# Two layers of three-way attention and a recurrent block on one core: the drains of queries, keys and gates are split in two

## The chip, the cores and the metric

The kernel runs on one core of one Trainium2 chip. The metric is the device time of one execution in microseconds. Engines are named by what they do: TensorE (PE in the rows; its weight loads are PEld), VectorE (DVE), ScalarE (ACT), GpSimd (POOL) and SyncE (SP). TensorE writes into PSUM, which this kernel uses as eight banks of 128 x 512 f32.

## The reference, cut to what matters

x is 512 tokens by 1024. Two layers run a projection into queries, keys, values and gates for three kinds of attention, each gated by silu, and a projection back; then a second block with a linear recurrence, dilated attention and a feed-forward part follows, which the change doesn't touch.

```python
def hybrid_layer(x, w_in, f_bias, lam_vec, subln, w_out, g_pre, g_post, layer_idx, cos, sin):
    h = rms_norm(x, g_pre)
    p = h @ w_in
    qa, ka, va, ga, qs, ks, vs, gs, qf, kf, vf, gf, ff = jnp.split(p, split_at, axis=-1)
    ...
    ya = merge(diff_attention(qa, ka, heads(va, ...), lam, lambda_init, subln))
    ya = ya * jax.nn.silu(ga)
    yb = merge(stick_breaking_attention(heads(qs, ...), heads(ks, ...), heads(vs, ...)))
    yb = yb * jax.nn.silu(gs)
    ...
    yc = merge(forgetting_attention(heads(qf, ...), heads(kf, ...), heads(vf, ...), cum_log_f))
    yc = yc * jax.nn.silu(gf)
    y = jnp.concatenate([ya, yb, yc], axis=-1) @ w_out
    return x + rms_norm(y, g_post)
```

## The kernel before

All heavy products are "dense groups". A group multiplies 512 tokens by a weight panel into four tiles of 128 x 512, one in each of the banks 0 to 3. It consists of blocks of 256 rows of the weights; every f32 operand is held as a high and a low part, so a block takes three products for each of its two row chunks and each tile, 24 in all (L644 to L646 with the tokens, L647 to L649 with the weights held in the array). A block's weights come by DMA on SyncE's queue, ScalarE makes the high part (L899) and GpSimd the low part (L627), two blocks ahead.

When the last block of a group is done the group is *drained*: ScalarE and, for some groups, VectorE read the four banks. For queries and keys of the kinds sb and fox (tag `qk`, two groups of four tiles a kind: query pair, key pair, query pair, key pair) ScalarE copies the high part (`qk_high`, L1013 and L1016) and VectorE then subtracts it to get the low part (`qk_low`, L1368 and L1372) and frees the bank. For gates (tag `g`) ScalarE alone applies silu (L980); that needs another activation table than the attention around it, so a table load stands before the first gate, and L1003 loads the attention's table back behind the last. The next group's first product into a bank waits until that bank is free.

The order of the work on every engine comes from one list of steps, `STEPS`, written by `plan()`; each engine walks the list and issues its part of each step, in order. `weave` mixes the blocks of the dense groups, cut into halves of two tiles (tiles 0 and 1, tiles 2 and 3), with the half-steps of an attention. Attention step n has part 0 (scores of unit n into banks 4 and 5, softmax or sticks, turning of unit n - 1, map 0) and part 1 (turning of unit n - 1, map 1, and at some steps the heads). Turned probabilities all pass one bank, 6 (`BT`): TensorE turns into it (L771), ScalarE copies the high part (L1069), VectorE subtracts the low part (L1463) and frees it, and only then TensorE may turn the next. In the kind diff ScalarE copies alone (L1075), exponentials are L1051, the combination L1452. Outputs pass one bank as well, 7 (`BO`): products with the values (L788), the turning of the heads (L823), and VectorE's `y_tmp` (L1532), which frees it for the next. L813 are row factors of fox, and need bank 7 too.

The fourteen groups that the change concerns are, in each of the two layers, `g` of the kinds diff, sb and fox, and `qk` m=0 and m=1 of sb and fox. The time in the trace of layer 0 is given beside them: g diff 118 us, qk sb m=0 198, qk sb m=1 257, g sb 290, qk fox m=0 320, qk fox m=1 390, g fox 433. Layer 1 follows 502 us later.

Of the kernel before, what the change touches and what calls it, by code (L numbers as in the profile page):

```python
# [40 lines left out]

HEADS_AT = {"diff": (10, 13, 16, 18), "sb": (11, 12, 14, 17), "fox": (13, 14, 15, 17), "dil": (8, 13, 17, 18)}
ATT_STEPS = {"diff": 19, "sb": 18, "fox": 18, "dil": 19}
NORM_CHUNKS = (range(DC // 2), range(DC // 2, DC))
S0, S1, BT, BO = 4, 5, 6, 7
MASKS = ("causal", "strict", "chunk", "prev", "mod4d", "mod4", "mod16d", "mod16")
# [2 lines left out]
def plan():  # L49

    groups, steps, blocks = [], [], []

    def dense(tag, rows, orient, **more):

        g = dict(tag=tag, n=rows // BC, orient=orient, index=len(groups), first=len(blocks), **more)
        groups.append(g)
        out = []
        for k in range(g["n"]):
            out.append(("block", len(blocks), len(groups) - 1, k, (0, 1, 2, 3)))
            blocks.append((len(groups) - 1, k))  # L60
        out.append(("drain", len(groups) - 1))
        return out

    def weave(segments, others):

        out, at = [], 0
        for dense_steps, upto in segments:
            rest = [half for st in dense_steps
                    for half in ([st[:4] + ((0, 1),), st[:4] + ((2, 3),)] if st[0] == "block" else [st])]
            n, seen = sum(st[0] == "block" for st in rest), 0  # L70
            for i, other in enumerate(others[at:upto]):
                while rest and (seen < math.ceil(n * (i + 1) / (upto - at)) or rest[0][0] != "block"):
                    seen += rest[0][0] == "block"
                    out.append(rest.pop(0))
                out.append(other)
            out += rest
            at = upto
        return out
# [106 lines left out]
    for st in steps:  # L185
        if st[0] == "drain":
            g = groups[st[1]]
            for j in range(4):
                take(("dense", st[1], j), j, signal=j < 3)
                if g["tag"] == "qk" and g["orient"] == "feat":  # L190
                    mark("qk_high", (st[1], j))
                if g["tag"] == "v" and g["kind"] != "diff":
                    mark("v_high", (st[1], j))
        elif st[0] == "normturn":
            for c in NORM_CHUNKS[st[2]]:
                take(("norm", st[1], c), 4 + c % 4)
        elif st[0] == "forget":
            take(("ff", st[1]), S0)
        elif st[0] == "ropeturn":
            for j in range(4):  # L200
                take(("rope", st[1], j), 4 + j)
                if groups[st[1]]["tag"] == "qk":
                    mark("qk_high", (st[1], j))
        elif st[:2] == ("lru", "decide"):
            take(("r", st[2]), 4 + 2 * (st[2] % 2))
            take(("i", st[2]), 5 + 2 * (st[2] % 2))
        elif st[0] == "att":
            _, l, kind, n, part = st
            turn, value = n - 1, n - 2
            if 0 <= turn < 16:  # L210
                for a in value_maps(kind):
                    if (a > 0) == part:
                        take(("T", l, kind, turn, a), (BT, 0, 1)[a] if kind == "dil" else BT)
                        if kind in ("sb", "fox"):
                            mark("p_high", (l, kind, turn, a))
            if n < 16 and part == 0:
                for a in unit_maps(kind):
                    take(("S", l, kind, n, a), (S0, S1, 3)[a])
                if kind in ("diff", "fox"):
                    for a in range(2):  # L220
                        mark("rows_max", (l, kind, n, a))
                if kind == "dil":
                    mark("rows_max", (l, kind, n, 0))
                if kind == "sb":
                    for a in range(2):
                        mark("sticks", (l, kind, n, a))
                if kind == "diff":
                    mark("soft", (l, kind, n, 1))
            if kind in ("sb", "fox"):
                for p, a in pair_at(n, part):  # L230
                    use[("map", l, kind, p, a)] = maps
                    maps += 1
                    take(("O", l, kind, p, a), BO, signal=False)
                    mark("y_half", (l, kind, p, a))
            elif 0 <= value < 16 and part == 0:
                for a in value_maps(kind):
                    use[("map", l, kind, value, a)] = maps
                    maps += 1
                take(("O", l, kind, value), BO, signal=False)
                if kind == "diff":  # L240
                    mark("rms", (l, kind, value))
            if kind == "fox" and factors_at(n, part) is not None:
                take(("R", l, kind, factors_at(n, part)), BO)
            if n in HEADS_AT[kind] and part == 1:
                p = HEADS_AT[kind].index(n)
                if kind in ("sb", "fox"):
                    mark("gated", (l, kind, p))
                else:
                    take(("Y", l, kind, p), BT if kind == "dil" else BO)
                mark("y_high", (l, kind, p))  # L250
                mark("y_low", (l, kind, p))
# [28 lines left out]
def build(nc, x, wstream, w_ff, f_bias, lam_vec, subln, gains, post_gains, masks, ident_in, sel_in, rope1, positions,  # L280
# [255 lines left out]
    def values_before(gi):  # L536

        n = 0
        for st in STEPS:
            if st == ("drain", gi):  # L540
                return n
            if st[0] == "att" and st[2] in ("sb", "fox"):
                n += len(pair_at(*st[3:]))
            elif st[0] == "att" and 0 <= st[3] - 2 < 16 and st[4] == 0:
                n += len(value_maps(st[2]))
# [48 lines left out]
    with nc.Block() as block:  # L594
# [290 lines left out]
        def _(act):  # L885
# [60 lines left out]
                act.wait_ge(s_lam_dots, l + 1)  # L946
                nc.scalar.activation(lam[:, 2:4], lam[:, 0:2], ACT.Exp).then_inc(s_lam_exp, 1)

            def drain(gi):
                g = GROUPS[gi]  # L950
                tag = g["tag"]
                if tag in ("o", "mix", "o2", "down"):
# [8 lines left out]
                        act.wait_ge(*full(("rope", before[-1], 3)))  # L961
                if tag == "g" and (g["l"], g["ki"]) != (0, 0):
                    act.wait_ge(s_y_low, MARKS["y_low", prev_kind(g["l"], g["kind"]) + (3,)])
                for j in range(4):
                    act.wait_ge(*tile_full(gi, j))
                    ps = bank[j]
                    done = freed(("dense", gi, j))
# [195 lines left out]
            for st in STEPS:  # L1163
# [1 line left out]
                    if st[4][0] == 0:  # L1165
                        high(st[1] + 2)
                elif st[0] == "drain":
                    drain(st[1])
                    if st[1] + 1 in LAST:
                        first_half(LAST.index(st[1] + 1))  # L1170
                elif st[0] == "norm":
# [58 lines left out]
        def _(dve):  # L1230
# [72 lines left out]
                    .then_inc(s_ck_ready, 1)  # L1303
                dve.wait_ge(s_ck_ready, l + 1)

            def drain(gi, tiles=range(4)):
                g = GROUPS[gi]
                tag = g["tag"]
                if tag == "qk" and g["orient"] == "feat":
                    for j in range(4):  # L1310
                        qk_low(g, j, ("dense", gi, j))
                    return
                if tag == "v" and g["kind"] != "diff":
# [327 lines left out]
            for st in STEPS:  # L1641
                if st[0] == "drain":
                    if st[1] not in LAST:
                        drain(st[1])
                elif st[0] == "norm":
                    norm(st[1])
                elif st[0] == "normturn":
# [160 lines left out]
```

## Time and profile before

| what | value |
|---|---|
| median of 3 runs | 1998.19 us (1995.54 to 2000.15) |
| the profiled execution | 1998.55 us, its span 1996.7 us |
| TensorE, busy | 1897.4 us, 95% of the span |
| ScalarE, busy | 906.2 us, 45% |
| VectorE, busy | 778.3 us, 39% |
| GpSimd, busy | 661.8 us, 33% |
| mean granted clock of TensorE | 0.988 |

The busy time of TensorE counts pipelined products whose ends are modelled, so 95% is not 95% of its peak. A row's idle time is the time in which the engine stood still just before, and behind the arrow stands what it was waiting for. Two products that follow each other without a wait start 0.23 us apart at 512 columns and full clock.

### The profile page before, as it was taken

The numbers are of one execution on the slowest core, as the hardware profiler recorded it, in microseconds if no ns is written. First come the engines' busy times: TensorE is split into PE (matmuls) and PEld (weight loads), VectorE is DVE, ScalarE is ACT, GpSimd is POOL, SyncE is SP. The second block draws the span as 40 slices with busy tenths as digits, with TensorE's granted clock in tenths as the row PEclk, the third lists the DMA queues.
The fourth block names the chain that finished last, engine by engine and source line by source line (L and its number), as shares of the span: only waits on it lengthen the run. The fifth ranks groups of instructions, "written<-read, shape, count | busy, mean of one in ns | idle before, by whom it ended". The sixth has DMA issues, their size and how long they took to land.

```text
span 1996.7 us, 24926 instructions
## 1 busy us (share of the span) xinstructions
PE 1897.4 (95%) x9233; PEld 1546.8 (77%) x9239; DVE 778.3 (39%) x1346; ACT 906.2 (45%) x1775; POOL 661.8 (33%) x278
## 2 busy tenths in 40 slices
PE   8998999898999899989899999999999999999998
PEld 6887777676788777777676888888788878888886
DVE  3434655534543565544447672010350431111002
ACT  4555565543465556554353833233453353323222
POOL 2422333122242222322233444434103423444442
PEclk9998999999999899999999999999999999999999
DMA  4221212112322121211231222222102422222322
GB/s 153 85 74 43 74 65 74 53 43 106 116 85 66 51 72 66 74 53 43 104 138 65 95 95 95 86 94 89 60 1 75 142 78 97 95 95 95 99 101 85
DMA packets 44568, 163.74 MB, mean 82 GB/s; under 512 B 6192, under 2 KB 6448, under 8 KB 43824
## 3 DMA queue, kind: packets, MB, share of 16 engines
q1 hardware_dynamic: 42640, 148.65, 22.3%
q10 hardware_dynamic: 1824, 13.63, 1.8%
q8 instruction: 74, 1.21, 0.2%
q14 instruction: 30, 0.25, 0.0%
HBM read 155.97 MB, written 6.29 MB: 81 GB/s over the span
## 4 chain that ended last, share of the span: by engine, by line
PE 82%; DVE 9%; ACT 6%; issue 3%; DMA 0%; POOL 0%; DVEq 0%; ACTq 0%; POOLq 0%; SPq 0%
PE bank L644 12%; PE bank L646 12%; PE bank L645 12%; PE bank L647 10%; PE bank L649 10%; PE bank L648 10%; PE bank L771 2%; PE bank L788 2%; ACT q_dup L1013 2%; PE bank L749 1%; PE bank L747 1%; PE bank L750 1%; DVE y_tok L1398 1%; PE bank L735 1%; PE bank L708 1%
## 5 line engine op out<-in xcount | busy, mean ns | idle before, releaser
L627 POOL TENSOR_TENSOR w_hl<-w_raw,w_hl 128x1024 fp32r<-128x1024 f32 x274 | 661.6, 2419 | 1310.6 <-ACT w_hl L899 1310.0
L899 ACT ACTIVATE w_hl<-w_raw 128x1024 fp32r<-128x1024 f32 x274 | 287.6, 1058 | 343.7 <-DMA w_raw<-wstream 343.2
L644 PE MATMUL bank<-act_hl,w_hl 128*128 128x512 f32 x1056 | 428.4, 406 | 5.7 <-DVE q_low L1368 2.8
L646 PE MATMUL bank<-act_hl,w_hl 128*128 128x512 f32 x1056 | 415.4, 393 | 0.0
L645 PE MATMUL bank<-act_hl,w_hl 128*128 128x512 f32 x1056 | 415.1, 393 | 0.0
L647 PE MATMUL bank<-w_hl,act_hl 128*128 128x512 f32 x672 | 265.6, 395 | 6.1 <-DVE q_low L1368 4.0
L649 PE MATMUL bank<-w_hl,act_hl 128*128 128x512 f32 x672 | 262.3, 390 | 0.0
L648 PE MATMUL bank<-w_hl,act_hl 128*128 128x512 f32 x672 | 262.0, 390 | 0.0
L644 PEld LDWEIGHTS bank<-act_hl,w_hl 128*128 128x128 f32 x1056 | 201.1, 190 | 48.9 <-issue 5.7
L646 PEld LDWEIGHTS bank<-act_hl,w_hl 128*128 128x128 f32 x1056 | 200.2, 190 | 43.5
L645 PEld LDWEIGHTS bank<-act_hl,w_hl 128*128 128x128 f32 x1056 | 201.1, 190 | 40.3 <-issue 1.9
L647 PEld LDWEIGHTS bank<-w_hl,act_hl 128*128 128x128 f32 x672 | 126.3, 188 | 33.9 <-issue 4.9
L649 PEld LDWEIGHTS bank<-w_hl,act_hl 128*128 128x128 f32 x672 | 126.2, 188 | 26.7
L648 PEld LDWEIGHTS bank<-w_hl,act_hl 128*128 128x128 f32 x672 | 126.4, 188 | 24.9
L1069 ACT ACTIVATE pt_hl<-bank 128x512 fp32r<-128x512 f32 (+3 forms) x128 | 55.9, 437 | 177.8 <-PE bank L771 177.5
L1463 DVE TENSOR_TENSOR pt_hl<-bank,pt_hl 128x512 fp32r<-128x512 f32 (+3 forms) x128 | 62.6, 489 | 162.7 <-ACT pt_hl L1069 162.6
L771 PE MATMUL bank<-ident,probs 128*128 128x128 f32 x508 | 89.6, 279 | 29.7 <-DVE pt_hl L1463 29.7
L1424 DVE TENSOR_REDUCE nmax<-bank 128x1 f32<-128x512 f32 (+3 forms) x128 | 59.3, 488 | 89.9 <-PE bank L758 86.8
L771 PEld LDWEIGHTS bank<-ident,probs 128*128 128x128 f32 x508 | 59.3, 142 | 40.7 <-DVE pt_hl L1463 34.2
L1354 DVE TENSOR_TENSOR probs<-bank,probs 128x512 f32<-128x512 f32 x22 | 15.1, 688 | 186.7 <-PE bank L646 186.7
L1396 DVE TENSOR_TENSOR y_tok<-probs,rope 128x256 f32<-128x256 f32 x10 | 4.3, 426 | 196.0 <-ACT probs L969 196.0
L1051 ACT ACTIVATE probs<-bank,nmax 128x256 f32<-128x256 f32 (+3 forms) x144 | 73.2, 515 | 14.8 <-DVE nmax L1424 14.0
(232 smaller groups left out, 2839.7 us busy)
## 6 DMA issues: line engine op xcount, KB each, us to landing
w_raw<-wstream SPq DMA_DIRECT2D x274, 512.0 KB, 3.5
x_spill<-x_res ACTq DMA_DIRECT2D x2, 2048.0 KB, 7.0
x_res<-x_spill ACTq DMA_DIRECT2D x2, 2048.0 KB, 7.9
x_res<-x SPq DMA_DIRECT2D x4, 512.0 KB, 5.7
g_post<-post_gains ACTq DMA_DIRECT2D x4, 512.0 KB, 3.6
x_res<-x ACTq DMA_DIRECT2D x1, 2048.0 KB, 8.4
out<-x_res SPq DMA_DIRECT2D x4, 512.0 KB, 2.6
probs<-w_gates ACTq DMA_DIRECT2D x1, 1024.0 KB, 10.7
```

Of the source, the lines that this page charges most:

```text
L627: nc.gpsimd.tensor_tensor(w_hl[:, slot, 1].rearrange("p c n -> p (c n)"), w_raw[:, slot, :], w_hl[:, slot, 0].rearrange("p c n -> p (c n)" ...
L644: pe.matmul(out_ap, wh, ah, start=start, stop=False)
L645: pe.matmul(out_ap, wh, al, start=False, stop=False)
L646: return pe.matmul(out_ap, wl, ah, start=False, stop=stop)
L647: pe.matmul(out_ap, ah, wh, start=start, stop=False)
L648: pe.matmul(out_ap, ah, wl, start=False, stop=False)
L649: return pe.matmul(out_ap, al, wh, start=False, stop=stop)
L771: tr = pe.transpose(to[:, kb * P:(kb + 1) * P], probs[:, p_slot(kind, n, a), kb * P:(kb + 1) * P], ident[:, :])
L899: nc.scalar.activation(w_hl[:, b % RING, 0].rearrange("p c n -> p (c n)"), w_raw[:, b % RING, :], ACT.Copy).then_inc(s_high_done, 1)
L1051: nc.scalar.activation(ps if in_bank else row, ps, ACT.Exp, bias=nmax[:, par, b:b + 1], accum_out=sums[:, par, a:a + 1])\
L1424: nc.vector.tensor_reduce(nmax[:, par, a:a + 1], ps[:, 0:nb * P], AX.X, ALU.max, negate=True)\
L1463: nc.vector.tensor_tensor(turned_part(1, a, i), ps.rearrange("p (k q) -> p k q", q=P), turned_part(0, a, i).bitcast(f32), ALU.subtract).th ...
```

## The change

The drain of a `qk` or `g` group inside a woven stretch is one step before. It becomes two: tiles 0 and 1 are drained right behind the half of the last block that fills them, before the attention half-step that stands between the block's halves; tiles 2 and 3 are drained behind the second half, where all four were drained before. Drains of other groups and outside `weave` stay whole.

```diff
+SPLIT_DRAINS = ("qk", "g")
...
-        out.append(("drain", len(groups) - 1))
+        out.append(("drain", len(groups) - 1, (0, 1, 2, 3)))
+        return out
+
+    def halves(st):
+
+        return [st[:-1] + ((0, 1),), st[:-1] + ((2, 3),)] if st[0] in ("block", "drain") else [st]
+
+    def halved(dense_steps):
+
+        out = []
+        for st in dense_steps:
+            if st[0] == "drain" and groups[st[1]]["tag"] in SPLIT_DRAINS:
+                first, second = halves(st)
+                out[-1:] = [first, out[-1], second]
+            else:
+                out += halves(st) if st[0] == "block" else [st]
         return out
...
-            rest = [half for st in dense_steps
-                    for half in ([st[:4] + ((0, 1),), st[:4] + ((2, 3),)] if st[0] == "block" else [st])]
+            rest = halved(dense_steps)
...
-            for j in range(4):
+            for j in st[2]:
                 take(("dense", st[1], j), j, signal=j < 3)
...
-            if st == ("drain", gi):
+            if st[:2] == ("drain", gi):
...
-            def drain(gi):
+            def drain(gi, tiles):
...
-                for j in range(4):
+                for j in tiles:
                     act.wait_ge(*tile_full(gi, j))
...
-                    drain(st[1])
+                    drain(st[1], st[2])
...
-            def drain(gi, tiles=range(4)):
+            def drain(gi, tiles):
...
-                    for j in range(4):
+                    for j in tiles:
                         qk_low(g, j, ("dense", gi, j))
```

The last lines of ScalarE's `drain`, which load the attention's table back behind the gates of a drain step, are not changed, so they run once for each of the two steps. TensorE's own order of instructions is the same before and after.

ScalarE at the gates of the kind diff in layer 0, before. L899 is the high part of a weight block, `gate` the gates from banks 0 to 3, L1075 the copy of turned probabilities in the attention step behind:

```order
L899 ACTIVATE w_hl_53<-w_raw_54 128x1024
L980 ACT_TABLE_LOAD
L980 ACTIVATE gate_63<-bank0 128x512
L980 ACTIVATE gate_63<-bank1 128x512
L980 ACTIVATE gate_63<-bank2 128x512
L980 ACTIVATE gate_63<-bank3 128x512
L1003 ACT_TABLE_LOAD
L1075 ACTIVATE probs_55<-bank6 128x128
```

The same place in the changed kernel, where the lines of the kernel have moved down by 15:

```order
L914 ACTIVATE w_hl_53<-w_raw_54 128x1024
L995 ACT_TABLE_LOAD
L995 ACTIVATE gate_63<-bank0 128x512
L995 ACTIVATE gate_63<-bank1 128x512
L1018 ACT_TABLE_LOAD
L995 ACT_TABLE_LOAD
L995 ACTIVATE gate_63<-bank2 128x512
L995 ACTIVATE gate_63<-bank3 128x512
L1018 ACT_TABLE_LOAD
L1090 ACTIVATE probs_55<-bank6 128x128
```

Nothing of the attention has moved between the halves here; a load back and a load forth stand between them.

VectorE at the queries and keys of sb, m=0, in layer 0 (the end of the diff attention), before. `y_tmp` is taken out of bank 7 for head 2 and, at the end, head 3:

```order
L1532 SCALAR_TENSOR_TENSOR y_tmp_58<-bank7,sub_g_94,gate_63 128x512
L1536 TENSOR_TENSOR y_hl_59<-y_tmp_58,y_hl_59 128x512
L1481 TENSOR_SCALAR y_tok_57<-bank7,stat_107 128x128
L1368 SCALAR_TENSOR_TENSOR q_low_67<-bank0,q_dup_64 64x512 x2
L1372 TENSOR_TENSOR k_hl_68<-bank1,k_hl_68 64x512 x2
L1368 SCALAR_TENSOR_TENSOR q_low_67<-bank2,q_dup_64 64x512 x2
L1372 TENSOR_TENSOR k_hl_68<-bank3,k_hl_68 64x512 x2
L1532 SCALAR_TENSOR_TENSOR y_tmp_58<-bank7,sub_g_94,gate_63 128x512
```

And in the changed kernel:

```order
L1383 SCALAR_TENSOR_TENSOR q_low_67<-bank0,q_dup_64 64x512 x2
L1387 TENSOR_TENSOR k_hl_68<-bank1,k_hl_68 64x512 x2
L1547 SCALAR_TENSOR_TENSOR y_tmp_58<-bank7,sub_g_94,gate_63 128x512
L1551 TENSOR_TENSOR y_hl_59<-y_tmp_58,y_hl_59 128x512
L1496 TENSOR_SCALAR y_tok_57<-bank7,stat_107 128x128
L1383 SCALAR_TENSOR_TENSOR q_low_67<-bank2,q_dup_64 64x512 x2
L1387 TENSOR_TENSOR k_hl_68<-bank3,k_hl_68 64x512 x2
L1547 SCALAR_TENSOR_TENSOR y_tmp_58<-bank7,sub_g_94,gate_63 128x512
```

The low parts of tiles 0 and 1 have moved ahead of head 2's `y_tmp`.

ScalarE at the queries and keys of fox, m=1, in layer 0, before. `pt_hl` are copies of turned probabilities out of bank 6, `raw_fox` half of an output out of bank 7, `probs` exponentials:

```order
L899 ACTIVATE w_hl_53<-w_raw_54 128x1024
L1069 ACTIVATE pt_hl_56<-bank6 128x512
L1091 ACTIVATE raw_fox_66<-bank7 64x512
L1069 ACTIVATE pt_hl_56<-bank6 128x3x128
L1051 ACTIVATE probs_55,sums_108<-bank4,nmax_109 128x256
L1051 ACTIVATE probs_55,sums_108<-bank5,nmax_109 128x256
L1013 ACTIVATE q_dup_64<-bank0 64x512 x4
L1016 ACTIVATE k_hl_68<-bank1 64x512 x2
L1013 ACTIVATE q_dup_64<-bank2 64x512 x4
L1016 ACTIVATE k_hl_68<-bank3 64x512 x2
L1069 ACTIVATE pt_hl_56<-bank6 128x384
```

And in the changed kernel:

```order
L914 ACTIVATE w_hl_53<-w_raw_54 128x1024
L1028 ACTIVATE q_dup_64<-bank0 64x512 x4
L1031 ACTIVATE k_hl_68<-bank1 64x512 x2
L1084 ACTIVATE pt_hl_56<-bank6 128x512
L1106 ACTIVATE raw_fox_66<-bank7 64x512
L1084 ACTIVATE pt_hl_56<-bank6 128x3x128
L1066 ACTIVATE probs_55,sums_108<-bank4,nmax_109 128x256
L1066 ACTIVATE probs_55,sums_108<-bank5,nmax_109 128x256
L1028 ACTIVATE q_dup_64<-bank2 64x512 x4
L1031 ACTIVATE k_hl_68<-bank3 64x512 x2
L1084 ACTIVATE pt_hl_56<-bank6 128x384
```

Six activations have moved ahead of two copies of turned probabilities, a half output and the exponentials; six stay ahead of the third copy.

## Rows read from the trace of the kernel before

**Rows 1.** The page, part 4: the chain that ended last, by engine.
```profile
PE 82%; DVE 9%; ACT 6%; issue 3%; DMA 0%; POOL 0%; DVEq 0%; ACTq 0%; POOLq 0%; SPq 0%
```

**Rows 2.** TensorE's waits over the span: us in total, times, longest.
```profile
PE bank L647 <- DVE q_low L1368: 8.4, 8, 1.6
```

**Rows 3.** Groups by line and shape: xcount, busy us, mean ns, idle before.
```profile
L1013 ACT ACTIVATE q_dup<-bank 64x512 fp32r<-64x512 f32 x96 | 56.8, 592 | 13.7 <-PE bank L735 12.5
...
L1372 DVE TENSOR_TENSOR k_hl<-bank,k_hl 64x512 fp32r<-64x512 f32 x48 | 33.0, 688 | 1.1
```

**Rows 4.** Timeline at the diff gates: start us, us, engine, line, idle before.
```profile
121.70 0.60 ACT L980 ACTIVATE gate<-bank 128x512 f32<-128x512 f32 x1 [0.40 <-PE bank L646]
122.31 1.28 ACT L1003 ACT_TABLE_LOAD   x1
123.61 0.28 ACT L1075 ACTIVATE probs<-bank 128x128 f32<-128x128 f32 x1
...
127.05 0.44 PE L749 MATMUL bank<-k_hl,q_dup 128*128 128x384 f32 x1 [0.54 <-DVE probs L1452]
```

**Rows 5.** Timeline at the queries and keys of sb, m=0.
```profile
193.71 1.05 ACT L899 ACTIVATE w_hl<-w_raw 128x1024 fp32r<-128x1024 f32 x1
...
196.08 0.75 DVE L1532 SCALAR_TENSOR_TENSOR y_tmp<-bank,sub_g,gate 128x512 f32<-128x512 f32 x1 [1.82 <-PE bank L823]
...
196.88 0.49 PE L788 MATMUL bank<-vv,probs 128*128 128x128 f32 x2 [0.84 <-DVE y_tmp L1532]
...
202.20 0.47 PE L647 MATMUL bank<-w_hl,y_hl 128*128 128x512 f32 x1 [1.64 <-DVE q_low L1368]
```

**Rows 6.** Timeline at the queries and keys of sb, m=1.
```profile
257.14 0.49 ACT L1069 ACTIVATE pt_hl<-bank 128x384 fp32r<-128x384 f32 x1 [0.50 <-PE bank L771]
...
260.24 0.39 PE L771 MATMUL bank<-ident,probs 128*128 128x128 f32 x2
261.50 0.47 PE L644 MATMUL bank<-act_hl,w_hl 128*128 128x512 f32 x1 [0.87 <-DVE q_low L1368]
...
265.06 0.50 PE L644 MATMUL bank<-act_hl,w_hl 128*128 128x512 f32 x1 [0.54 <-DVE q_low L1368]
```

**Rows 7.** Timeline at the queries and keys of fox, m=0.
```profile
319.32 0.60 ACT L1069 ACTIVATE pt_hl<-bank 128x512 fp32r<-128x512 f32 x1 [1.97 <-PE bank L771]
...
322.55 0.50 PE L771 MATMUL bank<-ident,probs 128*128 128x128 f32 x3
...
324.52 0.47 PE L647 MATMUL bank<-w_hl,act_hl 128*128 128x512 f32 x1 [1.48 <-DVE q_low L1368]
```

**Rows 8.** Timeline at the queries and keys of fox, m=1.
```profile
385.42 0.60 ACT L1069 ACTIVATE pt_hl<-bank 128x512 fp32r<-128x512 f32 x1 [1.80 <-PE bank L771]
...
386.80 0.55 PE L771 MATMUL bank<-ident,probs 128*128 128x128 f32 x3 [0.51 <-DVE pt_hl L1463]
...
399.12 0.69 PE L771 MATMUL bank<-ident,probs 128*128 128x128 f32 x2 [6.51 <-DVE pt_hl L1463]
```

**Rows 9.** Timeline at the fox gates.
```profile
432.65 0.38 ACT L1069 ACTIVATE pt_hl<-bank 128x256 fp32r<-128x256 f32 x1 [0.45 <-PE bank L771]
...
438.38 0.33 PE L771 MATMUL bank<-ident,probs 128*128 128x128 f32 x1 [1.34 <-DVE pt_hl L1463]
```

**Rows 10.** Windows: us; PE, PEld, DVE, ACT, POOL busy (x); clock, DMA, GB/s.
```profile
158.30:161.70 3.40, 1.18 (x11) 0.98 (x11) 1.53 (x6) 2.16 (x9) 1.65 (x1) 1.00 0.00 0
161.70:165.10 3.40, 3.40 (x12) 2.73 (x11) 1.44 (x2) 0.63 (x1) 0.00 (x0) 0.50 0.00 0
```

**Rows 11.** Timeline of TensorE behind the standstill of rows 8.
```profile
403.02 0.63 PE L646 MATMUL bank<-act_hl,w_hl 128*128 128x512 f32 x1
403.45 0.63 PE L644 MATMUL bank<-act_hl,w_hl 128*128 128x512 f32 x1
...
405.10 0.40 PE L646 MATMUL bank<-act_hl,w_hl 128*128 128x512 f32 x1
405.33 0.39 PE L644 MATMUL bank<-act_hl,w_hl 128*128 128x512 f32 x1
```

More of the change, by code:

```diff
@@ L1643, in _ @@
                     if st[1] not in LAST:
-                        drain(st[1])
+                        drain(st[1], st[2])
                 elif st[0] == "norm":
```

## The prediction

> **What bounds the kernel now.** I read the page's chain first: TensorE holds 82% of it and VectorE and ScalarE together 15% [rows 1]. So TensorE is the bound nearly everywhere, and a change can only win or lose where TensorE stands still. Then I read TensorE's waits and, in order of time, the places at which a split group is drained, seven a layer, fourteen in all. Eight waits of 8.4 us in total go to L647, a dense product, for the low half of the queries (L1368) [rows 2]: the next group cannot begin because ScalarE and VectorE have not yet emptied bank 0. That is what splitting would remove. The timelines show the price of a drain. One copy of a query tile is 0.592 us and a tile needs four, a key tile two of the same shape; each half-width subtraction on VectorE is 0.688 us and a tile needs two [rows 3]. So a query tile takes ScalarE 2.4 us, a key tile 1.2 us, and VectorE 1.4 us each. A table load takes 1.28 us [rows 4]. The two layers repeat each other, so I work out layer 0 and double it.
>
> **How I cost it.** Every instruction keeps its number and duration, except for table loads. What moves is the order on ScalarE and VectorE: tiles 0 and 1 are now drained ahead of an attention half-step, in the time of the 12 dense products (12 x 0.23 us = 2.75 us) that fill tiles 2 and 3. Both engines work their lists in order, so what stood ahead of the drain now stands behind half of it. For each place I take the time at which ScalarE is free after its weight copy (L899), lay the half drain there, and then follow who waits.
>
> **Gates, diff kind (layer 0: 118 to 127 us).** On ScalarE nothing lies between the two halves, so the split only adds a load back and a load forth: 2 x 1.28 us, less the 0.40 us which ScalarE now idles before the fourth tile: +2.16 us before L1075 and the exponentials [rows 4]. TensorE already waits 0.54 us for their result at 127.05 (L749 behind L1452) [rows 4]: the whole +2.16 lands on the path.
>
> **Gates, fox kind (429 to 441 us).** ScalarE is free at 432.20 (432.65 less its idle 0.45) [rows 9]. Load, two gates, load back end at 435.95; only then the turned probabilities (L1069, 0.38, before at 432.65) run, then load, two gates, load: the next L1069 starts at 440.1 instead of 437.73, and TensorE's L771, which stood 1.34 us at 438.38 [rows 9], goes at 440.75: +2.4 us, a standstill of 3.7 us.
>
> **Gates, sb kind.** The bank wait goes away, and as much comes back at L771 behind the delayed L1069. Laid out in the same way it nets to +0.15; the nearest waits for a bank and for L1463, 0.87 and 0.51 us, bound it at -0.9 and +0.5 [rows 6, 8].
>
> **Queries and keys, sb, first half (192 to 207 us).** ScalarE is free at 194.76, half drain to 198.4. VectorE, whose list had y_tmp (L1532) first, now does four subtractions first: from 197.2 to 200.0; y_tmp ends at 200.75 instead of 196.83 [rows 5]. TensorE's L788 waits for that, since y_tmp empties the bank of the attention outputs: it goes at 200.8 instead of 196.88, a standstill of 4.7 us where 0.84 stood [rows 5]. Behind it are 12 dense products and the heads' turning, 3.6 us, so the next group starts at 204.4 instead of 202.20 [rows 5]. It no longer stops inside, as it did for banks 2 and 3 (0.54 us for bank 2 in the like place of rows 6, some 0.3 for bank 3), since these are now free at 206.3 and 207.7, before it comes to them; that gives back 0.8 or 0.9. Net +1.3 us. Cover lost: y_tmp had nothing ahead of it.
>
> **Queries and keys, sb, second half (256 to 265 us).** ScalarE is free at 256.64 (257.14 less 0.50) [rows 6], half drain to 260.25, L1069 to 260.75; VectorE's key subtractions end at 261.85, its L1463 at 262.4. TensorE's L771 stood at 260.24 without a wait and now goes at 262.45; the dense product behind starts at 262.8 instead of 261.50 [rows 6], but its 0.54 us stop for bank 2 goes. Net +0.4.
>
> **Queries and keys, fox, first half (316 to 331 us).** Here ScalarE is free early, at 317.35: it idled 1.97 us before L1069 [rows 7]. Half drain to 321.0, L1069 to 321.6, VectorE's L1463 to 323.3: L771 goes at 323.35 instead of 322.55, the dense group at 323.8 instead of 324.52, and the stops inside of the kind in rows 6, again 0.8 or 0.9 us, vanish [rows 6, 7]: -1.6.
>
> **Queries and keys, fox, second half (380 to 400 us).** ScalarE is free at 383.62 (385.42 less 1.80) [rows 8]. L1463 for turn 4 ends at 389.6, so L771, before at 386.80, goes then, and the block behind is 2.8 us later. Its fill of tile 2 starts the second half drain: 2.4 us copies of queries, 1.2 keys, then VectorE's remainder and L1463, to 398.7 instead of 399.12, where TensorE stood 6.51 us [rows 8]. Two standstills of about 3.3 us in place of one of 6.5: -0.4.
>
> Sum for a layer: 2.16 + 2.4 + 0.15 + 1.3 + 0.4 - 1.6 - 0.4 = 4.4 us; two layers +8.8 us.
>
> **The clock.** The granted clock went from 1.00 (2.4 GHz) to 0.50 (1.2 GHz) after a stretch of 3.40 us in which TensorE was busy 1.18 us, and stayed for 3.4 us [rows 10]; after the 6.51 us standstill dense products follow at 0.43 us and then, back at full clock, at 0.23 us [rows 11]. At the lower level 3.4 us of dense work lose 3.4 x (1 - 0.23/0.43) = 1.6 us. After the shorter bank waits of rows 5 and 6 it did not fall. So the new 4.7 us standstill should bring a fall, the 3.7 us one too, the one at the diff gates (0.7 + 2.2 us) half the time: 2 x (1.6 + 1.6 + 0.8) = +8 us. At the fox keys two short falls replace one long: 0. Bounds: 0 if none falls, +14 if all do. I take +8: 1998.6 (the profiled execution, 0.4 above the median of the three runs, 1998.2) + 8.8 + 8 = **2015 us**.
>
> **A rule weighed.** The trace has the table load at 1.28 us and the next instruction 0.02 us behind it (122.31 to 123.61), with the gate just ahead ending at 122.30 [rows 4]. The Trainium skill (ScalarE: Activation LUTs, "What ACT_TABLE_LOAD costs") adds a drain of about 1.38 us to every switch. By the row two more loads cost 2.57 us. By the page they would cost 5.3, and the eight on the path some 11 us more than in my sum. The trace speaks against the page here: no gap of that size stands on either side of the load.
>
> **Rivals.**
> 1. Faster (12%). The half drain fits into ScalarE's idle time before L1069, as at fox first half, at the other three places too, since nobody needs L1463 or y_tmp at once. Then the 8.4 us of bank waits go, and the fox keys' 6.5 us shrinks by the 3.6 us of the first half in each layer; the loads stay, 2 x 4.6: -8.4 - 7.2 + 9.2 = -6.4, about 1992. For it: ScalarE idles 0.5 to 2 us before L1069 [rows 6 to 8]. Against it: VectorE ends 1.6 us behind ScalarE, and L788 stood behind y_tmp already [rows 5]. It decides at whether the delayed L1463 or y_tmp ends before TensorE has done its 2.75 us.
> 2. No change (12%). The doubled loads are hidden by attention's own slack, the queries and keys net to (1.3 + 0.4 - 1.6 - 0.4) x 2 = -0.6, and only the 4.7 us standstill costs two falls, 3.2: about 2001. Against it: at both gate places TensorE already waits for ScalarE's chain [rows 4, 9].
> 3. Every extra load brings a second part of its own length in which ScalarE's pipe empties, 1.28 us more at most by the row: 2 loads x 4 places on the path: +10, about 2025 (4%). The page named above says so, with 1.38.
> My forecast: 72%.
>
> **How the numbers follow.** A measurement of this kernel tells about 0.2%, 4 us. The forecast's own range is 2006 to 2024: 8.8 with 3 us of error in my laying out, and 0 to 14 for the clock. The range, 1999 to 2023, leaves out rival 1, most of 3 and the edges. Faster 0.12; within 0.2% 0.13; slower 0.75, which is the forecast less its lowest edge, and rival 3.
>
> **What would show it.** In the profile after: 12 more table loads; the waits of L647 and L644 for q_low gone or nearly; a wait of L788 for y_tmp of about 4.7 us twice; L771 waiting for L1463 with maxima of 3 to 4 us instead of 6.5, and more often; the clock at 0.50 shortly after the first. I would be wrong if VectorE took y_tmp or L1463 before the half drain, if L771's total did not rise, or if the clock stayed at full behind these standstills.

## The result, and the profile after

| what | before | changed |
|---|---|---|
| median of 4 runs each, interleaved on one chip | 1999.17 us (1995.54 to 2000.85) | 2015.06 us (2013.1 to 2016.27) |
| ratio, 95% interval | | 1.0086 [1.0073, 1.0099] |
| span of the profiled execution | 1996.7 us | 2012.3 us |
| mean granted clock of TensorE | 0.988 | 0.982 |

The change makes the kernel 0.86% slower by the ratio; the two medians lie 15.9 us (0.79%) apart. The forecast was 2015 us.

The page after, the shares of the chain by engine, then busy time and instructions of each engine:

```profile
PE 81%; DVE 9%; ACT 6%; issue 3%; DMA 0%; POOL 0%; DVEq 0%; ACTq 0%; POOLq 0%; SPq 0%
...
PE 1904.0 (95%) x9233; PEld 1553.7 (77%) x9239; DVE 777.1 (39%) x1346; ACT 922.3 (46%) x1787; POOL 663.0 (33%) x278
```

This page alone would hardly tell that anything happened: TensorE still holds 81% of the chain, against 82% [rows 1], and 1904.0 us busy against 1897.4 is work of the same products at a lower clock. ScalarE has 16 us more, which is the table loads. What moved stands in TensorE's waits (us in total, times, longest):

```profile
PE bank L786 <- DVE pt_hl L1478: 38.7, 26, 3.5
...
PE bank L803 <- DVE y_tmp L1547: 9.4, 2, 4.7
```

Before, the waits of the same kinds that were not shown yet:

```profile
PE bank L771 <- DVE pt_hl L1463: 29.7, 20, 6.5
...
PE bank L644 <- DVE q_low L1368: 2.8, 4, 0.9
PE bank L788 <- DVE y_tmp L1532: 1.7, 2, 0.8
```

Lines are 15 further down after, L786 and L803 being L771 and L788. The bank waits for the low queries [rows 2] are gone. In their place L803 stands twice for `y_tmp`, 4.7 us each time, where all waits of that kind were 1.7 us before, and the turning of probabilities, 29.7 us before, stands 38.7 us, with a maximum of 3.5 instead of 6.51 [rows 8]. So 11.2 us of bank waits for the low queries (8.4 at L647 and 2.8 at L644) were taken away and 7.7 + 9.0 = 16.7 us of waits for the attention put there. Smaller waits moved too, those of the diff gates above all. All in all TensorE's idle time, the span less the busy time, went from 99.3 us to 108.3 us, and its busy time grew by 6.6 us; together that is the 15.6 us by which the span grew.

The groups of instructions by line and form (xcount, busy us, mean ns, idle before) show the loads. Before:

```profile
L980 ACT ACT_TABLE_LOAD x6 | 7.7, 1283 | 0.1
L1003 ACT ACT_TABLE_LOAD x6 | 7.7, 1283 | 0.1
```

And after:

```profile
L995 ACT ACT_TABLE_LOAD x12 | 15.4, 1283 | 0.2
L1018 ACT ACT_TABLE_LOAD x12 | 15.4, 1283 | 0.2
```

The timeline after (start us, length, engine, line, operation, idle before and what ended it), from the diff gates to the fox gates of layer 0. These rows answer to rows 4 to 9:

```profile
119.89 1.28 ACT L995 ACT_TABLE_LOAD   x1
...
122.29 1.28 ACT L1018 ACT_TABLE_LOAD   x1
123.58 1.28 ACT L995 ACT_TABLE_LOAD   x1
...
125.97 1.28 ACT L1018 ACT_TABLE_LOAD   x1
127.27 0.28 ACT L1090 ACTIVATE probs<-bank 128x128 f32<-128x128 f32 x1
128.27 0.44 PE L764 MATMUL bank<-k_hl,q_dup 128*128 128x384 f32 x1 [0.69 <-ACT probs L1066]
...
130.71 0.44 PE L764 MATMUL bank<-k_hl,q_dup 128*128 128x384 f32 x1 [1.75 <-DVE probs L1467]
...
199.58 1.39 DVE L1383 SCALAR_TENSOR_TENSOR q_low<-bank,q_dup 64x512 fp32r<-64x512 f32 x2 [2.82 <-ACT q_dup L1028]
201.01 1.39 DVE L1387 TENSOR_TENSOR k_hl<-bank,k_hl 64x512 fp32r<-64x512 f32 x2
202.43 0.75 DVE L1547 SCALAR_TENSOR_TENSOR y_tmp<-bank,sub_g,gate 128x512 f32<-128x512 f32 x1
203.23 0.79 PE L803 MATMUL bank<-vv,probs 128*128 128x128 f32 x2 [4.70 <-DVE y_tmp L1547]
...
267.68 0.44 PE L786 MATMUL bank<-ident,probs 128*128 128x128 f32 x2 [2.01 <-DVE pt_hl L1478]
...
330.63 0.55 PE L786 MATMUL bank<-ident,probs 128*128 128x128 f32 x3 [0.82 <-DVE pt_hl L1478]
330.93 0.47 PE L662 MATMUL bank<-w_hl,act_hl 128*128 128x512 f32 x1
...
395.11 0.90 PE L786 MATMUL bank<-ident,probs 128*128 128x128 f32 x3 [3.35 <-DVE pt_hl L1478]
...
405.60 0.69 PE L786 MATMUL bank<-ident,probs 128*128 128x128 f32 x2 [3.47 <-DVE pt_hl L1478]
...
446.40 0.47 PE L786 MATMUL bank<-ident,probs 128*128 128x128 f32 x1 [3.53 <-DVE pt_hl L1478]
```

Three readings. At 199.58 VectorE has stood for ScalarE's query copies with `y_tmp` behind it in its list; four subtractions run, `y_tmp` comes at 202.43 and TensorE at 203.23. At 330.93 the dense product follows without a stop, where it stood 1.48 us before [rows 7]. And at 395.11 and 405.60 two waits of 3.4 us stand in place of one of 6.51 [rows 8].

TensorE issues the same products in the same order in both kernels, so each instruction has a lateness, its start after minus its start before. Read at the places of the change it says where the time went:

| layer 0, place | start before | start after | late | grown by |
|---|---|---|---|---|
| first dense products behind the start | 110.03 | 111.51 | 1.48 | 1.48 |
| diff gates, scores behind the combination | 127.05 | 130.71 | 3.66 | 2.18 |
| ahead of sb m=0 | 195.44 | 197.94 | 2.50 | -1.16 |
| sb m=0, values for `y_tmp` | 196.88 | 203.23 | 6.35 | 3.85 |
| sb m=0, behind it | 209.13 | 214.61 | 5.48 | -0.87 |
| ahead of sb m=1 | 256.62 | 261.88 | 5.26 | -0.22 |
| sb m=1, L786 | 260.24 | 267.68 | 7.44 | 2.18 |
| sb m=1, behind it | 267.96 | 275.03 | 7.07 | -0.37 |
| fox m=0, L786 | 322.55 | 330.63 | 8.08 | 1.01 |
| fox m=0, behind it | 330.98 | 336.49 | 5.51 | -2.57 |
| fox m=1, first wait | 386.80 | 395.11 | 8.31 | 2.80 |
| fox m=1, behind the second | 404.42 | 410.09 | 5.67 | -2.64 |
| fox gates, L786 | 438.38 | 446.40 | 8.02 | 2.35 |
| fox gates, behind it | 442.93 | 452.47 | 9.54 | 1.52 |

At 500 us the lateness is 8.4, at 1010 us 15.3 and at the end 15.6. Without the 1.5 us of the start each layer adds 6.9 us: layer 1 repeats layer 0, and behind the two layers next to nothing is added.

The windows after (us; busy us of PE, PEld, DVE, ACT, POOL and instructions; granted clock, DMA share, GB/s) at six places where the clock was at 0.50, the one at the start first, then behind sb m=0, sb m=1, the two waits of fox m=1 and the fox gates:

```profile
16.20:19.60 3.40, 3.37 (x8) 2.72 (x9) 0.79 (x2) 1.65 (x2) 2.61 (x2) 0.50 0.33 136
...
200.50:207.40 6.90, 4.17 (x11) 3.39 (x12) 3.64 (x6) 2.53 (x8) 0.00 (x0) 0.51 0.00 0
...
268.80:272.20 3.40, 3.40 (x10) 2.62 (x9) 3.27 (x8) 2.66 (x8) 0.62 (x1) 0.50 0.01 2
...
395.10:398.50 3.40, 3.39 (x13) 3.01 (x14) 2.07 (x5) 1.51 (x5) 0.00 (x0) 0.50 0.02 5
405.30:408.75 3.45, 3.15 (x9) 2.57 (x10) 1.82 (x6) 2.14 (x6) 0.05 (x1) 0.51 0.00 0
446.30:449.70 3.40, 3.30 (x11) 3.01 (x12) 0.84 (x4) 2.72 (x7) 1.15 (x1) 0.50 0.02 5
```

The falls at 200, 268 and 446 us are new; the two at fox m=1 stand for one of 6.8 us before. At the diff gates there is none in this execution. Up to the last stretch, some 6 us at 0.50 with which both kernels end, the clock was at 0.50 for 64.8 us, against 41.0 before.

### The profile page after: what moved, and what is told of

Its sections match the earlier page's. It is cut to its first block, busy times and chain, and to the rows that moved or that the text cites. A ratio compares the mean times of both kernels' runs of the same rounds, so it can differ in the third digit from the quotient of the medians.

```text
span 2012.3 us, 24943 instructions
## 1 busy us (share of the span) xinstructions
PE 1904.0 (95%) x9233; PEld 1553.7 (77%) x9239; DVE 777.1 (39%) x1346; ACT 922.3 (46%) x1787; POOL 663.0 (33%) x278
## 4 chain that ended last, share of the span: by engine, by line
PE 81%; DVE 9%; ACT 6%; issue 3%; DMA 0%; POOL 0%; DVEq 0%; ACTq 0%; POOLq 0%; SPq 0%
PE bank L659 12%; PE bank L661 12%; PE bank L660 12%; PE bank L662 10%; PE bank L664 10%; PE bank L663 10%; PE bank L786 2%; PE bank L803 2%; PE bank L764 1%; PE bank L762 1%; PE bank L765 1%; DVE y_tok L1413 1%; ACT q_dup L1028 1%; ACT probs L1066 1%; PE bank L750 1%
## 5 line engine op out<-in xcount | busy, mean ns | idle before, releaser
L786 PE MATMUL bank<-ident,probs 128*128 128x128 f32 x508 | 91.1, 282 | 38.7 <-DVE pt_hl L1478 38.7
L1478 DVE TENSOR_TENSOR pt_hl<-bank,pt_hl 128x512 fp32r<-128x512 f32 (+3 forms) x128 | 62.6, 489 | 167.6 <-ACT pt_hl L1084 167.0
L786 PEld LDWEIGHTS bank<-ident,probs 128*128 128x128 f32 x508 | 59.8, 144 | 51.3 <-DVE pt_hl L1478 44.9
```

The costliest lines, as they stand in the source:

```text
L786: tr = pe.transpose(to[:, kb * P:(kb + 1) * P], probs[:, p_slot(kind, n, a), kb * P:(kb + 1) * P], ident[:, :])
L1478: nc.vector.tensor_tensor(turned_part(1, a, i), ps.rearrange("p (k q) -> p k q", q=P), turned_part(0, a, i).bitcast(f32), ALU.subtract).th ...
```

## The experiments

Nine kernels were run, each with its profile, and each against the kernel before on the same chip (three rounds for e1 to e4, five for the others).

| kernel | median us | before, same chip | ratio, 95% | worth against before |
|---|---|---|---|---|
| e1 gates alone split | 2010.77 | 1998.59 | 1.0056 [1.0039, 1.0073] | +11.2 |
| e2 queries and keys alone split | 2005.63 | 1998.59 | 1.0032 [1.0019, 1.0044] | +6.4 |
| e3 changed, no load back between halves | 2003.07 | 1998.59 | 1.0021 [1.0011, 1.0031] | +4.2 |
| e4 changed, sb m=0 whole | 2009.93 | 1998.59 | 1.0053 [1.0036, 1.0070] | +10.6 |
| e5 changed, filler ahead of the 4.7 us wait | 2010.15 | 1998.18 | 1.0059 [1.0046, 1.0073] | +11.8 |
| e6 fox m=0 alone split | 1992.80 | 1998.18 | 0.9971 [0.9961, 0.9982] | -5.8 |
| e7 fox m=0 split, fox m=1 split late | 1987.32 | 1998.18 | 0.9944 [0.9931, 0.9958] | -11.2 |
| e8 fox m=1 split late alone | 1992.94 | 1998.36 | 0.9974 [0.9963, 0.9984] | -5.2 |
| e9 fox m=0 alone split, again | 1992.04 | 1998.36 | 0.9971 [0.9962, 0.9980] | -5.8 |

The last column is the ratio less 1, times some 1998.3 us, and its uncertainty 2 to 3.5 us. On the same scale the change itself is +17.2.

### e1 and e2: which half of the change costs

```diff
-SPLIT_DRAINS = ("qk", "g")
+SPLIT_DRAINS = ("g",)
```

> Only the drains of the gates are split; queries and keys are drained whole, as before. My theory (the two extra table loads of 1.28 us land on the path at the diff and the fox gates, and the 3.7 us standstill at the fox gates brings a fall of the clock): 2 x (2.2 + 0 + 2.3) + 2 x 1.5 = +12 us on the kernel before, about 2010. Rival (the loads are hidden by the attention's slack and all of the loss is in the queries and keys): within 2 us of before.

```diff
-SPLIT_DRAINS = ("qk", "g")
+SPLIT_DRAINS = ("qk",)
```

> Only the drains of queries and keys are split; the gates are drained whole, as before. My theory: a layer gives +3.1 at sb m=0 (of it 1.8 from the clock), +1.4 at sb m=1, -1.4 at fox m=0, +0.3 at fox m=1, so +5 to +7 us on the kernel before. Rival (the gates' loads make all of the loss): within 2 us of before, or faster by the bank waits, -8.

Measured +11.2 and +6.4. They add up to 17.6, and both together cost 17.2. TensorE's waits in e1:

```profile
PE bank L786 <- DVE pt_hl L1478: 35.4, 22, 6.5
...
PE bank L662 <- DVE q_low L1383: 8.5, 8, 1.6
```

And in e2:

```profile
PE bank L786 <- DVE pt_hl L1478: 33.7, 24, 3.3
...
PE bank L803 <- DVE y_tmp L1547: 9.4, 2, 4.7
```

With the gates alone the bank waits for the low queries and the longest wait of 6.5 us are what they were before; with the queries and keys alone these go and the two of 4.7 us come. So each wait belongs to the half that the forecast named. The gates also brought what the profile after did not have, a fall behind the diff gates, in both layers. The window of e1 in layer 0:

```profile
130.40:133.80 3.40, 3.40 (x13) 2.83 (x12) 1.33 (x5) 2.68 (x10) 1.62 (x1) 0.50 0.02 5
```

### e3: the loads themselves

In the diff and fox gates the table is left where it is between the halves: what runs there, if anything, is a copy, and the trace of e3 has no load next to it.

```diff
-                if tag == "g":
+                if tag == "g" and (g["kind"] == "sb" or 3 in tiles):
                     act.preload_act_table_set(
```

> The changed kernel, but at the diff and the fox gates the attention's table is loaded back only behind the second half (nothing of the attention between the halves needs it there; copies run with any table). At the sb gates it is still loaded back behind both. 8 table loads fewer than in the changed kernel. My theory (loads on the path): -2 x (2.2 + 2.2) and two falls of the clock gone, -2 x 1.4: about -11 us on the changed kernel, +4 on the kernel before. Rival (it is the place of the half drain, not the loads, that costs at the gates): within 3 us of the changed kernel.

Measured +4.2 against before, 13 us less than the change. The forms of e3, with eight loads of each kind:

```profile
L995 ACT ACT_TABLE_LOAD x8 | 10.3, 1283 | 0.1
L1018 ACT ACT_TABLE_LOAD x8 | 10.3, 1283 | 0.1
```

And its timeline at the diff gates, where the changed kernel stood 1.75 us:

```profile
129.31 0.44 PE L764 MATMUL bank<-k_hl,q_dup 128*128 128x384 f32 x1 [0.54 <-DVE probs L1467]
```

The stop is again the 0.54 us of before [rows 4]. Eight loads less, and the clock's falls behind them (e3 has none at either gate place), are worth 13 us. That is all that splitting the gates cost (+11.2 in e1), and 2 us more, which lies within the uncertainty. So at the gates the loads are the cause, not the split.

### e4: sb m=0 drained whole

```diff
+    def early(g):
+        return g["tag"] in SPLIT_DRAINS and (g["tag"], g["kind"], g["m"]) != ("qk", "sb", 0)
...
-            if st[0] == "drain" and groups[st[1]]["tag"] in SPLIT_DRAINS:
+            if st[0] == "drain" and early(groups[st[1]]):
```

> The changed kernel, but the queries and keys of sb m=0 are drained whole, as before. My theory (the half drain ahead of y_tmp makes TensorE stand 4.7 us for bank 7, and the clock falls behind it): -2 x 3.1 = -6 us on the changed kernel, L803 waiting under 1 us for y_tmp, and two falls of the clock fewer. Rival (the earlier free banks 0 and 1 give the standstill back): within 2 us of the changed kernel.

Measured +10.6, so 6.6 us less than the change. The timeline of e4 there:

```profile
200.24 0.49 PE L807 MATMUL bank<-vv,probs 128*128 128x128 f32 x2 [0.84 <-DVE y_tmp L1551]
...
205.57 0.47 PE L666 MATMUL bank<-w_hl,y_hl 128*128 128x512 f32 x1 [1.64 <-DVE q_low L1387]
```

Both stops are exactly those of before [rows 5], and the clock stays at 1.00 behind them. (In this execution it did fall at the diff gates, at 129.7 us, so that its span says less than the median.) 6.6 us for two such places is 3.3 each; the forecast had 1.3 for the order and 1.6 for the clock. The two parts are told apart by the next kernel.

### e5: the same wait, without the fall

The changed kernel, with 16 bf16 products of 512 columns into bank 4, which is idle there. They stand in step 17 of diff, behind the turning of probabilities and ahead of the output products that wait for `y_tmp`, and they begin once the last scores in bank 4 have been read. Nothing reads them.

```diff
+            def fill(l, n):
+                pe.wait_ge(*drained(("S", l, "diff", 15, 0)))
+                for _ in range(n):
+                    pe.matmul(bank[S0][:, :], mask_b[:, len(MASKS), :], ..., start=True, stop=True)
...
+                        if kind == "diff" and n == 17:
+                            fill(l, 16)
```

> The changed kernel with 16 products of bf16 constants, 512 columns each, on TensorE just before the output product of diff step 17, into bank 4, which is free there; their result is not used. They fill some 3.7 us of the 4.7 us standstill in each layer and change no wait. If the fall of the clock to 0.50 behind the standstill is what costs 1.6 to 1.9 us a layer there: -3 to -4 us on the changed kernel and the granted clock at 1.00 behind it. If the clock costs nothing there: within 1 us. If the products stand in the way of the output product: slower.

The timeline of e5 has the filler and the wait behind it:

```profile
199.46 3.40 PE L714 MATMUL bank<-mask_b 128*128 128x512 bf16 x15
...
204.09 0.49 PE L810 MATMUL bank<-vv,probs 128*128 128x128 f32 x2 [1.24 <-DVE y_tmp L1556]
```

And its window over that stretch:

```profile
198.80:206.40 7.60, 6.31 (x31) 3.86 (x31) 4.55 (x7) 4.67 (x11) 1.78 (x1) 1.00 0.00 0
```

TensorE goes on with the values when `y_tmp` lets it, as before, but the clock is at 1.00. Measured -5.4 us by the ratios, -4.0 by the spans of the profiled executions (2012.3 to 2008.3), for two places: 2 to 2.7 each, where the sum had 1.6. The ratios' uncertainty (3 us and more for their difference) leaves that open, but the trace of the changed kernel gives the size: the fall there lasted 6.8 us and not 3.4, 2.7 us of it over the standstill and 4.1 us over products, and under it the lateness grew from 6.35 to 8.27 us, in layer 1 from 13.23 to 15.11. That is 1.9 us a place. What is shown is that the wait costs twice: as a wait, and by the clock behind it.

### e6 and e9: the one place that gained

Only the fox group m=0 is drained in two; all others whole.

```diff
+        return g["tag"] in SPLIT_DRAINS and (g["tag"], g["kind"], g["m"]) == ("qk", "fox", 0)
```

> Only the queries and keys of fox m=0 are drained in two pieces; everything else as before. This is the one place where ScalarE idled 2 us before the turned probabilities and my sum had a gain. My theory: -1.4 x 2 = -3 us on the kernel before. Rival (a split of this kind never gains, the half drain costs what it frees): within 1 us or slower.

Measured -5.8, more than the -3. The timeline of e6, with the same 0.82 us as in the changed kernel:

```profile
323.52 0.55 PE L790 MATMUL bank<-ident,probs 128*128 128x128 f32 x3 [0.82 <-DVE pt_hl L1482]
```

TensorE's lateness is 0 at 319 us and -1.6 at 331, as forecast; then -2.3 at 404 and -3.9 at 475, -5.8 at the end. So nearly half of the gain came from places that the split does not touch. To see whether that is chance, the same kernel was run again.

> The same kernel as the one with fox m=0 alone, a second time, since it gained 5.8 us where the order of the work accounts for 2 x 1.4 to 1.6. If the rest is the clock's falls, which lie differently in every execution: between -3 and -6 us again, and a profile whose falls lie elsewhere. If it is a gain in the order that I have not seen: again -5.8, with the same steps of TensorE earlier.

-5.8 again, with the same picture. In the kernel before the clock falls behind a turn of the last fox steps, at 468.9 us:

```profile
468.90:472.30 3.40, 3.40 (x12) 2.92 (x11) 1.90 (x3) 0.59 (x1) 0.93 (x1) 0.50 0.00 0
```

In e9 (and e6) it does not, at the same work:

```profile
467.60:471.00 3.40, 3.25 (x17) 2.67 (x16) 0.58 (x1) 0.12 (x1) 0.00 (x0) 1.00 0.10 16
```

That is 1.6 us, in layer 0 alone; 0.7 more comes under the fall of fox m=1. e8, which is not split at fox m=0, has no fall there in layer 0 either. What spares that fall was not tried.

### e7 and e8: the fox group m=1 late

Before, ScalarE has all twelve copies of this group ahead of the third copy of turned probabilities, and the changed kernel puts six of them ahead of the first. Here tiles 0 and 1 are drained where the whole group was, and tiles 2 and 3 behind the attention half-step that comes next, so that copy stands between them. e7 has e6's edit as well.

```diff
+                split = st[0] == "drain" and [groups[st[1]].get(k) for k in ("tag", "kind", "m")] == ["qk", "fox", 1]
-                out += halves(st) if st[0] == "block" else [st]
+                out += halves(st) if st[0] == "block" or split else [st]
...
+        for st in [st for st in out if st[0] == "drain" and st[2] == (2, 3)]:
+            if groups[st[1]]["m"] == 1:
+                i = out.index(st)
+                out[i:i + 2] = [out[i + 1], st]
```

> As the kernel with fox m=0 alone, and the queries and keys of fox m=1 are drained in two pieces too, but with the second piece later instead of the first piece earlier: tiles 0 and 1 where all four were drained before, tiles 2 and 3 behind the next half-step, so the third turned map no longer stands behind all of the drain. My theory: the 6.5 us standstill shrinks to about 2.8 and the fall of the clock behind it goes or halves: -3 for fox m=0 and -2 x (3.7 + 1 to 2) for fox m=1, together -13 us on the kernel before. Rival (the standstill moves to bank 2 or 3 of the next group): -3 us, as with fox m=0 alone.

Measured -11.2, 1987.32 us: 0.56% faster than the kernel before and the fastest version of this study. The timeline of e7:

```profile
389.65 2.40 ACT L1037 ACTIVATE q_dup<-bank 64x512 fp32r<-64x512 f32 x4
392.08 1.20 ACT L1040 ACTIVATE k_hl<-bank 64x512 fp32r<-64x512 f32 x2
393.30 0.49 ACT L1093 ACTIVATE pt_hl<-bank 128x384 fp32r<-128x384 f32 x1
393.68 2.39 ACT L1037 ACTIVATE q_dup<-bank 64x512 fp32r<-64x512 f32 x4
395.54 0.69 PE L795 MATMUL bank<-ident,probs 128*128 128x128 f32 x2 [2.88 <-DVE pt_hl L1487]
```

The copy `pt_hl` stands between the two halves, and TensorE waits 2.88 us for its low part where it waited 6.51 [rows 8]. TensorE's waits of this kind over the span:

```profile
PE bank L795 <- DVE pt_hl L1487: 25.4, 24, 2.9
```

25.4 us against 29.7 before and 38.7 after. A fall of the clock is still there behind it, half as long as the one of 6.8 us before; the window of e7:

```profile
395.40:398.80 3.40, 3.26 (x9) 2.68 (x10) 2.73 (x6) 2.23 (x5) 0.00 (x0) 0.50 0.00 0
```

The late split was then run without e6's edit.

> The later second piece at the queries and keys of fox m=1 alone; fox m=0 is drained whole again. If the two splits add up, this is the kernel with both less the one with fox m=0 alone: -11 + 5.5, so -5 to -8 us on the kernel before, about 1991. By my own sum (3.7 us of standstill a layer and part of a fall of the clock) -9 to -10. Rival (the gain needs fox m=0 too, since the moved falls of the clock made it): under 3 us.

Measured -5.2. The wait in its timeline is that of e7:

```profile
396.40 0.44 PE L795 MATMUL bank<-ident,probs 128*128 128x128 f32 x2 [2.89 <-DVE pt_hl L1487]
```

-5.8 and -5.2 make -11.0, and both together gave -11.2: the two edits add up. The sum by which the late split alone should have brought 9 to 10 us fell: 3.6 us less of waiting a layer is 7.2 us, and part of it comes back at the next turned probabilities, whose copy on ScalarE now stands behind the second half drain. TensorE did not stand there before; in e8 it does, in both layers (at 899.58 us in layer 1):

```profile
401.58 0.61 PE L795 MATMUL bank<-ident,probs 128*128 128x128 f32 x2 [2.00 <-DVE pt_hl L1487]
```

In e7, where the products ahead of this place ran at the lower clock, the same wait is 0.50 us.

## Why the prediction was right

The sign, the size and the main waits were right. That the sum met 2015.06 us to a tenth is luck: its terms were off by up to 3 us for the two layers, and the errors cancelled. By the steps of the sum, read in layer 0:

- **Diff gates, +2.16.** The lateness grew by 2.18 at the place named, 0.69 and 1.75 us of waits in place of 0.54. e3 shows that it is the loads.
- **sb m=0, +1.3 and a fall of 1.6.** The standstill is 4.70 us, as forecast, and the lateness grew by 3.85 - 0.87 = 2.98 against 2.9. Of this 1.9 is the fall and 1.1 the order. e4 gives 3.3 a place; e5 shows that the fall is a part of it.
- **sb m=1, +0.4.** L786 came 2.18 later, where 2.21 was worked out (262.45 less 260.24), and 1.8 of it was given back by the bank stops that went, so the order's +0.4 is met. But the clock fell at 268.8, behind a wait of 2.01 us, and under it the lateness grew from 6.38 to 7.80, by 1.4. Together the place cost +1.8 instead of +0.4. The step that failed is that this place, with a wait of two microseconds, was left out of the clock's list. e2 and e3 have the same wait of 2.02 us in both layers and no fall behind it, so here the term would be a part of 1.4, not the whole.
- **sb gates, +0.15.** The lateness was 7.07 at 290 us, ahead of it, and 7.08 at 300 us, behind it.
- **fox m=0, -1.6.** 7.07 to 5.51 is -1.56; e6 gives the same at the place alone.
- **fox m=1, -0.4.** L786 came 2.80 later at the first wait (2.8 worked out), and 5.51 to 5.67 over both is +0.2. The two falls of 3.4 us for one of 6.8 were foreseen.
- **Fox gates, +2.4 and a fall of 1.6.** 2.35 and then 1.52, after a wait of 3.53 (3.7 worked out).
- **Order, +8.8, and clock, +8.** TensorE's idle time grew by 9.0 us, which answers to the order, and its busy time, with the same products, by 6.6 us, which answers to the clock. That second size is made of other items than the forecast's: no fall at the diff gates in this execution (but two in e1), one at sb m=1 that was not listed, 1.9 instead of 1.6 at sb m=0, 1.2 given back at 178.8 us, where a fall of 6.8 us is 3.4 long after, and 1.5 lost at 16 us, ahead of every changed place.
- **Two slips in the working.** At sb m=1 the times given make 1.3 (262.8 less 261.50) less 0.54, so 0.8; +0.4 takes in the 0.3 for bank 3, which is named only at sb m=0. The lowest edge of the forecast by its own terms is 2004 (1998.6 + 8.8 - 3), not 2006, and the +14 for the clock is not worked out. None of this moves the result.
- **The rule weighed.** The load takes 1.283 us, and what follows stands 0.01 us behind (122.29 + 1.28, then 123.58; before, 123.61 [rows 4]). Two more loads moved TensorE by 2.18 us, not by 5. So the drain that the Trainium skill (ScalarE: Activation LUTs, "What ACT_TABLE_LOAD costs") adds to a switch is not seen here.

Of the rivals, the first (faster) failed at its own condition: at all four places the delayed L1478 or `y_tmp` ended behind TensorE's 2.75 us. But at fox m=0 it ended only 0.82 us behind, less than the 1.48 us of the bank wait that went, and e6 makes this place a gain: 5.8 us, of which 2 x 1.6 are the order. The second (loads hidden) is ruled out by e1, +11.2, and e3. The third (a drain behind each load) would have made 2025 us; it is ruled out by the rows above and by the measured 2015.06 us.

The expectations for e1, e2 and e4 came out within 1 us or so of what was measured, that for e3 within 2 (-13 on the changed kernel for -11), those for e5 to e7 within 1 to 3. For e8 the adding of two runs held (-5 to -8) and the own sum was off by 4.

## What to carry to other kernels

Draining a group earlier frees its banks earlier, but on engines that work in order it also pushes what TensorE needs next behind it. Of the four places of queries and keys here it gained at the one where ScalarE stood idle for 2 us ahead of that step (fox m=0). It lost most where bank 7 is handed on behind the drain (`y_tmp`, sb m=0): there the new wait, with the clock, cost 3 us more than the bank waits that it removed. At fox m=1 it paid to put the second half behind the hand-over of bank 6 instead of the first ahead of it (e7, e8); at sb m=0 and m=1 that was not tried. And a cut must not fall between two switches of a resource: splitting a gate drain doubled its table loads, and these made the cost of the gates (e1, e3).

## What the runs showed of the hardware

- The same standstill may or may not be followed by a fall of the clock. At the diff gates the clock stayed at 1.00 after 0.69 + 1.75 us of waits in the changed kernel and in e5, and fell in e1, which has the same order there; in e4 it fell in layer 0 and not in layer 1. That is 3 of 8 times. Behind the wait of 2.0 us at sb m=1 it fell 4 of 10 times (the changed kernel, e2 to e5), behind the 3.5 us at the fox gates 8 of 8 (the changed kernel, e1, e4, e5), and at the 4.7 us of sb m=0 6 of 6 (the changed kernel, e2, e3). At the start, where no kernel differs, five of the nine experiments have a fall at 15 to 17 us as the changed kernel has, and the kernel before and the other four have none. A span of one profiled execution thus carries 1.5 us and more of chance, which is why the sizes above come from the ratios where they can.
- Small shifts of time go with other falls elsewhere: 2 to 3 us earlier at that point, e6 and e9 have no fall near 469 us in layer 0, both times, and that gains as much there as the split itself.
- 16 bf16 products of 512 columns, issued where TensorE would have stood for 4.7 us, kept the clock at 1.00 and gave back 4.0 to 5.4 us for two places (e5).
- A table load took 1.283 us and the instruction behind it began 0.01 to 0.02 us later, whether that was another load (at 123.58 us in the changed kernel) or an activation (at 124.87 us).
